# Two-stream transformer blocks in split float32: modulation slabs in a ring of their own, and both halves of the rows in one 512-column product

## The chip, the cores and the metric

One core of a Trainium2 chip runs the kernel. The metric is the device time of one execution in microseconds. The kernel before took 2739.88 us (median of 3 runs, 2738.51 to 2742.72).

## What is computed

Two blocks of two layers each, over 256 latent rows (`x`) and 256 context rows (`ctx`) of width 1024, all in float32. The first block, cut to what matters:

```python
for l in range(2):
    m_lat = split(silu(c) @ ada_w[l] + ada_b[l], 6)          # the same for ctx from c_ctx
    h_lat, h_ctx = modulate(x_lat, m_lat[0], m_lat[1]), modulate(x_ctx, m_ctx[0], m_ctx[1])
    y = even_mixer(...) if l == 0 else odd_mixer(...)        # attentions, then @ w_out
    x_lat = layer_norm(ALPHA * x_lat + m_lat[2] * y_lat, ln_g[l, 0], ln_b[l, 0])
    f = conv_ffn(modulate(x_lat, m_lat[3], m_lat[4]), ...)   # @ w_up, width-3 conv, silu(g) * a, @ w_down
    x_lat = layer_norm(ALPHA * x_lat + m_lat[5] * f, ln_g[l, 1], ln_b[l, 1])
    # x_ctx likewise, in layer 0 only
```

The second block takes these rows and a second context. Each of its layers has RMS norms and modulation with rows of its own, a mixer that adds three gated branches (a 31-tap convolution, differential attention `a = p0 - lam * p1; a @ v`, a multiscale pool), then `@ w_out` and a gated feed-forward `(silu(g) * a) @ w_down`. In layer 0 of each block both streams are computed (512 rows), in layer 1 the latent rows alone (256). The output is the 256 latent rows.

## The kernel before

**Layout.** Activations lie feature by feature: a chunk is 128 features by up to 512 rows. A linear is a list of groups; one group makes 128 output features of all rows in one PSUM bank, from 8 chunks of input (22 in the `down` linears). `plan_linears` writes the order of all linears by hand; `Linear` holds name, groups, tiles to a slab and rows `n`.

**Split products.** Weights and activations are float32, and each is split into a high part, rounded to the matmul's `fp32r`, and a low part, the rest. A product is three matmuls into one bank, high x high, low x high and high x low (lines 570 to 572):

```python
pe.matmul(out, wh[:, cols], high, start=first, stop=False)
pe.matmul(out, wh[:, cols], low, start=False, stop=False)
ins = pe.matmul(out, wl[:, cols], high, start=False, stop=last)
```

**Weights.** SP loads slabs (512 KB, 8 tiles of 128x128; 6 or 5 tiles in `down`) in the order of the plan into a `ring` of four slots. It asks for slab n when slab n-4 has been multiplied (line 526). For each slab ACT copies the high part (line 984) and VectorE subtracts for the low part (line 1617); both do so two slabs ahead (`ahead`, called by `turns` before a group's body). Where the next linear of the plan is one of modulation rows, the look ahead ends, and `begin` makes its successor's first two slabs: in `modulate` at step 3 (`BEGIN`) for `up2_0` and `up2_1`, after the attention for `branch_0` and `branch_1`.

**Groups.** Groups alternate between banks 0 and 1. A body on ACT or VectorE waits for `slab_done`, empties the bank and raises `emptied`; TensorE waits for that before it uses the bank again. `gated` with `residual` serves `mix1` and `down1`, `plain` serves `out` and `down2`, `silu_half`, `high_hidden` and `hidden` serve `up2`. The first two groups of a linear (`opening`) run side by side, chunk by chunk, as their inputs arrive.

**Modulation.** The rows `silu(c) @ w` come in parts named block_layer_part, each 16 slabs of 512 KB. `mod_slab` multiplies one (line 618): four float32 products of 256 columns in four column groups of the array. A part is then copied (`mod_copy`, line 1035), turned by TensorE (`mod_turn`, line 641) and stored with its bias (`mod_store`, line 1634); `stored` makes TensorE wait for that. Parts 1_0_1 and 1_0_2 run between the units of attention `global`, 1_1_0 and 1_1_1 in `near`, 1_1_2 and 2_0_0 in `window`, 2_0_1 and 2_0_2 in `diff_0`, 2_1_1 in `diff_1`. 2_1_0 is multiplied between `out_0` and `up2_0`, 2_1_2 between `out_1` and `up2_1`, through the same ring of four slots. `mods_until` spreads the slabs over the units.

**Attention.** `attend` exists on three engines. A unit is a head pair (or, in `diff`, a head's two maps) by 128 queries: TensorE makes scores (line 719), VectorE the row maxima (1858), ACT the exponentials with their sums (1270), VectorE scales by the reciprocals (1877, 1878; in `diff` 1880 to 1882), TensorE transposes (729), ACT copies (1281), TensorE multiplies by the values (742, 744), VectorE stores (1886). TensorE runs its scores two units ahead, and its modulation slabs between scores and transposes.

**Seams.** After `mix1_0` comes the layer norm `first_norm`: the sum of rows, centring (1717), squares (1059), their sum by TensorE (649), root (1064), reciprocal (1782), then for each chunk the norm (1819), gain and modulation (1241 on ACT, 1822 on VectorE), the high half (1234) and the low half (1663). After `out_0` and `out_1` comes `square_stat`, a root and reciprocal, the update of X (2210, 2215), squares (1564) with TensorE's sums of them (649), a second root and reciprocal, and `modulate` (1676, 1101, 1112, 1694). There TensorE's order is written out by hand: two slabs, `square_stat`, six slabs, then a sum and a slab in turn, eight times.

## Time and profile before

| | |
|---|---|
| median of 3 runs | 2739.88 us |
| the profiled execution | 2742.61 us |
| its span, first to last instruction | 2740.8 us |
| mean granted TensorE clock over the span | 0.974 |
| TensorE busy, share of the span | 94% |
| VectorE, ACT, GpSimd busy | 60%, 46%, 8% |
| DMA, mean over the span | 144 GB/s |

Busy time of TensorE counts every matmul from its start to its modelled end, and matmuls overlap: where they follow each other, the distance of two starts is the cost of one, not its duration. A float32 matmul (scores, slabs, transposes, sums) shows as two records, an `fp32r` one as one. The name before a line number is the engine, then output<-inputs by the kernel's names. In brackets stands the idle time of the engine before the row, and what ended it.

From the first product of a linear to its last, by the timeline, in us:

| stretch | from | to |
|---|---|---|
| attentions `global`, `near` | 151.5 | 282.18 |
| `mix1_0` | 282.18 | 328.31 |
| `up1_0` | 347.65 | 598.19 |
| attention `window` | 777.66 | 856.69 |
| `up1_1` | 921.74 | 1051.70 |
| `down1_1` | 1052.06 | 1116.19 |
| attention `diff_0` | 1465.01 | 1556.68 |
| `out_0` | 1655.88 | 1699.65 |
| `up2_0` | 1738.32 | 1979.03 |
| attention `diff_1` | 2354.91 | 2409.86 |
| `out_1` | 2473.98 | 2499.63 |
| `up2_1` | 2531.51 | 2660.77 |
| `down2_1` | 2661.13 | 2724.78 |

### The profile page before, as it was taken

How to read it: one execution, taken by the hardware profiler on the slowest of the kernel's cores; microseconds unless marked ns; L12 is line 12 of the kernel's file. 1: busy time of each engine (PE TensorE's matmuls, PEld its weight loads, DVE VectorE, ACT ScalarE, POOL GpSimd, SP SyncE). 2: the span in 40 equal slices, each digit the busy share in tenths (PEclk: the TensorE clock that was granted, in tenths of full speed). 3: DMA queues.
4: the chain of work that ended last, by engine and by line, in shares of the span. 5: the costliest groups of instructions: out<-in, count | busy, mean ns of one | idle time of the engine just before them, and what ended most of it. 6: DMA issues, size and time to landing. Idle time of an engine off the chain costs nothing.

```text
span 2740.8 us, 43247 instructions
## 1 busy us (share of the span) xinstructions
PE 2564.3 (94%) x16774; PEld 2154.4 (79%) x16774; DVE 1635.2 (60%) x2702; ACT 1274.2 (46%) x2372; POOL 209.5 (8%) x218
## 2 busy tenths in 40 slices
PE   7989889999988999999999999899999999987997
PEld 4744668888956899988875686588889999685997
DVE  2466465553687686668756763433326788764554
ACT  3355353433656665633336733422235644753443
POOL 3000100001201000324000001000001130000000
PEclk9999999999999999999999999999999999998999
DMA  7267222324554455534324433323245555445555
GB/s 277 86 228 270 72 66 95 99 88 127 164 190 157 149 182 172 175 101 146 115 92 143 140 100 135 125 93 99 88 112 162 170 172 175 154 135 200 176 173 142
DMA packets 119418, 393.64 MB, mean 144 GB/s; under 512 B 13728, under 2 KB 15776, under 8 KB 119136
## 3 DMA queue, kind: packets, MB, share of 16 engines
q1 hardware_dynamic: 117392, 386.47, 44.2%
q0 software_dynamic: 1872, 5.02, 0.7%
q8 instruction: 108, 1.77, 0.3%
q14 instruction: 46, 0.38, 0.0%
HBM read 390.39 MB, written 1.05 MB: 143 GB/s over the span
## 4 chain that ended last, share of the span: by engine, by line
PE 81%; DVE 9%; ACT 4%; DMA 4%; issue 1%; POOL 1%; SPq 0%; ACTq 0%; DVEq 0%; POOLq 0%
PE bank L570 23%; PE bank L571 23%; PE bank L572 23%; PE bank L719 2%; DMA ring<-in_w_mod 2%; PE bank L618 2%; DVE w_low L1617 2%; PE bank L729 2%; PE bank L649 1%; ACT w_high L984 1%; PE bank L744 1%; PE bank L742 1%; DVE smax L1858 1%; DVE conv_space L2118 1%; PE bank L679 1%
## 5 line engine op out<-in xcount | busy, mean ns | idle before, releaser
L570 PE MATMUL bank<-h_high,w_high 128*128 128x256 f32 (+1 forms) x3168 | 1058.4, 334 | 72.7 <-DVE w_low L1617 36.7
L1617 DVE TENSOR_TENSOR w_low<-ring,w_high 128x1024 fp32r<-128x1024 f32 (+2 forms) x604 | 684.1, 1134 | 610.5 <-ACT w_high L984 608.6
L572 PE MATMUL bank<-h_high,w_low 128*128 128x256 f32 (+1 forms) x3168 | 1041.1, 329 | 0.0
L571 PE MATMUL bank<-h_low,w_high 128*128 128x256 f32 (+1 forms) x3040 | 997.5, 328 | 0.0
L570 PEld LDWEIGHTS bank<-h_high,w_high 128*128 128x128 f32 x3168 | 610.8, 193 | 135.1 <-issue 58.3
L984 ACT CAST w_high<-ring 128x1024 fp32r<-128x1024 f32 (+2 forms) x604 | 574.1, 953 | 284.2 <-DMA ring<-in_w_down 161.6
L572 PEld LDWEIGHTS bank<-h_high,w_low 128*128 128x128 f32 x3168 | 610.7, 193 | 51.0
L571 PEld LDWEIGHTS bank<-h_low,w_high 128*128 128x128 f32 x3040 | 585.9, 193 | 48.9 <-issue 0.7
L570 PE MATMUL bank<-f_high,w_high 128*128 128x256 f32 (+1 forms) x880 | 269.2, 306 | 2.7 <-DVE w_low L1617 2.5
L571 PE MATMUL bank<-f_low,w_high 128*128 128x256 f32 (+1 forms) x880 | 267.7, 304 | 0.0
L572 PE MATMUL bank<-f_high,w_low 128*128 128x256 f32 (+1 forms) x880 | 267.6, 304 | 0.0
L570 PEld LDWEIGHTS bank<-f_high,w_high 128*128 128x128 f32 x880 | 168.1, 191 | 10.9 <-DVE w_low L1617 3.6
L571 PEld LDWEIGHTS bank<-f_low,w_high 128*128 128x128 f32 x880 | 168.1, 191 | 7.0
L572 PEld LDWEIGHTS bank<-f_high,w_low 128*128 128x128 f32 x880 | 168.1, 191 | 6.9
L1270 ACT ACTIVATE h_space<-bank,smax 128x512 f32<-128x512 f32 (+1 forms) x192 | 116.3, 610 | 88.8 <-DVE smax L1858 88.5
L2118 DVE SCALAR_TENSOR_TENSOR conv_space<-big,vec,conv_space 128x512 f32<-128x512 f32 (+1 forms) x240 | 150.4, 672 | 1.3
L1389 ACT ACTIVATE conv_space<-bank,vec 128x512 f32<-128x512 f32 (+1 forms) x88 | 59.1, 672 | 180.3 <-PE bank L572 179.1
L1858 DVE TENSOR_REDUCE smax<-bank 128x1 f32<-128x512 f32 (+1 forms) x192 | 108.5, 598 | 40.0 <-PE bank L719 37.0
L618 PE MATMUL bank<-ring,cvec_padded 128*8 128x256 f32 x1408 | 103.5, 392 | 17.7 <-DMA ring<-in_w_mod 16.0
L2011 DVE SCALAR_TENSOR_TENSOR conv_space<-bank,vec,conv_space 128x510 f32<-128x510 f32 (+1 forms) x88 | 54.2, 616 | 102.8 <-ACT conv_space L1389 102.8
L618 PEld LDWEIGHTS bank<-ring,cvec_padded 128*8 128x8 f32 x1408 | 25.4, 88 | 105.2 <-issue 57.3
L570 PE MATMUL bank<-o_halves,w_high 128*128 128x512 f32 (+1 forms) x256 | 91.3, 357 | 13.1 <-DVE w_low L1617 6.7
(230 smaller groups left out, 2625.2 us busy)
## 6 DMA issues: line engine op xcount, KB each, us to landing
ring<-in_w_mod SPq DMA_DIRECT2D x176, 512.0 KB, 4.4
ring<-in_w_up SPq DMA_DIRECT2D x176, 512.0 KB, 3.5
ring<-in_w_down SPq DMA_DIRECT2D x80, 384.0 KB, 3.1
ring<-in_w_down SPq DMA_DIRECT2D x80, 320.0 KB, 3.0
ring<-in_w_gate SPq DMA_DIRECT2D x48, 512.0 KB, 3.5
ring<-in_w_k SPq DMA_DIRECT2D x32, 512.0 KB, 3.5
ring<-in_w_v SPq DMA_DIRECT2D x32, 512.0 KB, 3.5
ring<-in_w_q SPq DMA_DIRECT2D x24, 512.0 KB, 3.5
```

Of the source, the lines that this page charges most:

```text
L570: pe.matmul(out, wh[:, cols], high, start=first, stop=False)
L571: pe.matmul(out, wh[:, cols], low, start=False, stop=False)
L572: ins = pe.matmul(out, wl[:, cols], high, start=False, stop=last)
L618: ins = pe.matmul(bank[b][32 * q:32 * q + MOD_ROWS, 0:256], padded[:, first:first + MOD_ROWS], slab[:, 256 * q:256 * (q + 1)], start=(k == ...
L719: pe.matmul(banks[(2 * u + i) % 4][:, 0:units[u]["T"]], q, k, start=True, stop=True).then_inc(sc_done, 1)
L729: ins = pe.transpose(bank[5 + k % 2][:, t * P:(t + 1) * P], src[:, t * P:(t + 1) * P], IDENT)
L984: nc.scalar.copy(wh[:, cols], raw[:, cols]).then_inc(high_ready, 1)
L1270: nc.scalar.activation(PROB[j % 6][:, 0:unit["T"]], banks[j % 4][:, 0:unit["T"]], ACT.Exp, bias=m, accum_out=ssum[:, j % NS:j % NS + 1]).t ...
L1389: nc.scalar.activation(SC[:, at.u, 0:w], bank[at.u % 2][:, 0:w], ACT.Identity, scale=vcol(l, at.g + (V1["conv_w"] + 2 * FC)), bias=vcol(l, ...
L1617: v.tensor_tensor(wl[:, cols], raw[:, cols], wh[:, cols].bitcast(F32), ALU.subtract).then_inc(low_ready, 1)
L1858: ins = v.reduce_max(m, sc[:, 0:w], AX_X, negate=True)
L2118: ins = v.scalar_tensor_tensor(cvs(c), U[:, c, 0:ns, k:k + S], vcol(l, V2["conv_w"] + c * CONV_TAPS + k), cvs(c), ALU.mult, ALU.add)
```

## The change

**A second ring.** `spare`, eleven slots of a slab in the region that the gates and hidden rows use at other times, takes the slabs of four modulation parts: 1_1_0, which leaves `near`; 2_1_1, which leaves `diff_1`; 2_1_0 and 2_1_2. `plan_spare` gives each slab a slot and names the ring load behind which SP issues it. 1_1_0 is multiplied between `mix1_0` and `up1_0`, 2_1_0 and 2_1_1 between `out_0` and `up2_0`, 2_1_2 where it was. 1_0_2 moves from `global` to `near`. Their turns and stores stand behind `up1_0` and `up2_0`, that of 2_1_2 between the sums.

**Casts ahead.** The four parts leave the plan, so `ahead` reaches from `out_0` and `out_1` into `up2`, and from `group_1` into `branch_1`; `BEGIN` goes. `branch_0`'s first slabs are made in the last unit of `diff_0`.

**`diff`.** The probabilities are `p0 + (s0 * -lam / s1) * p1`, and 1/s0 is applied when the output is stored.

**`first_norm`.** VectorE makes the low half of chunk c-2, not c-1, behind the norm of chunk c.

**Packed products.** In `down1_1`, `up2_1` and `down2_1` the high weights of all groups but the first two meet high and low rows, 256 each, in one product of 512 columns; low weights meet the high rows in the first 256 columns. ACT copies the second half of the bank out, VectorE adds it to the first, then the old body follows.

```diff
+        self.packed = name in ("down1_1", "up2_1", "down2_1")
...
-    modulation(1, 1, 0, 1)
+    modulation(1, 1, 1)
...
-        modulation(2, l, *((1, 2) if l == 0 else (1,)))
+        if l == 0:
+            modulation(2, l, 1, 2)
-        if l == 1:
-            modulation(2, 1, 2)
-        if l == 0:
-            modulation(2, 1, 0)
...
+SPARE = 11
+def plan_spare():
+    order, loads = {}, {}
+    uses, last = [0] * SPARE, [0] * SPARE
+    for parts, places in ((("1_1_0",), [("mix1_0", g, 3) for g in (4, 5, 6)] + [("mix1_0", 7, 2), ("up1_0", 3, 5)]),
+                          (("2_1_0", "2_1_1"), [("merge_0", g, 1) for g in (5, 6, 7)] +
+                           [("out_0", g, 2) for g in (4, 5, 6, 7)] + [("up2_0", 3, 21)]),
+                          (("2_1_2",), [("merge_1", g, 1) for g in (5, 6, 7)] +
+                           [("out_1", g, 2) for g in (4, 5, 6, 7)] + [("up2_1", 3, 5)])):
+        slabs = iter([(part, k) for part in parts for k in range(16)])
+        slot = 8
+        for name, g, count in places:
+            for _ in range(count):
+                one = next(slabs)
+                uses[slot] += 1
+                order[one] = (len(order) + 1, slot, uses[slot], last[slot])
+                last[slot] = len(order)
+                loads.setdefault((name, g), []).append(one)
+                slot = (slot + 1) % SPARE
+    return order, loads
+    SPARE_ORDER, SPARE_LOADS = plan_spare()
...
-    return min(slabs, u * slabs // (len(units) - 2))
+    return min(slabs, u * slabs // (len(units) - (2 if units[0]["diff"] else 0)))
...
+    for one in SPARE_LOADS.get((L.name, at.g), ()) if isinstance(at.g, int) else ():
+        _, slot, _, freed = SPARE_ORDER[one]
+        if freed:
+            sp.wait_ge(spare_done, freed)
+        sp.dma_start(spare[:, slot * SLAB * P:(slot + 1) * SLAB * P],
+                     T["w_mod" + one[0]][one[1] // 4, one[1] % 4]).then_inc(spare_landed[slot], 16)
...
-    if L.halved_at(at.u):
+    if side_by_side(at):
+        both = rhs(kc, at)
+        wide = bank[at.u % 2][:, 0:2 * L.n]
+        if first:
+            pe.matmul(wide, wh[:, cols], both, start=True, stop=False)
+            pe.matmul(out, wl[:, cols], both[:, 0, :], start=False, stop=False)
+        else:
+            pe.matmul(out, wl[:, cols], both[:, 0, :], start=False, stop=False)
+            ins = pe.matmul(wide, wh[:, cols], both, start=False, stop=last)
+    elif L.halved_at(at.u):
...
-        layer_norm(w)
+        spare_slabs("1_1_0", range(3))
+        row_stat(0, w, KC, 2)
+        spare_slabs("1_1_0", range(3, 5))
+        stat(lambda c: O[:, c, 0:w], KC, w, sq_ready, 3)
+        spare_slabs("1_1_0", range(5, 16))
-    linear(f"down1_{l}", of_f(w), arriving=(hid_ready, n["hid"]))
+    if l == 0:
+        mod_turn("1_1_0")
+    linear(f"down1_{l}", both_f if l == 1 else of_f(w), arriving=(hid_ready, n["hid"]))
+        stored()
...
+    def out_norm(c):
+        if l == 0 and c < 6:
+            spare_slabs("2_1_0" if c == 0 else "2_1_1", (15,) if c == 0 else (c - 1,))
+        elif l == 1 and c < 4:
+            spare_slabs("2_1_2", (12 + c,))
+        elif l == 1 and c == 6:
+            mod_turn("2_1_2")
-    mod_rows(part, range(2))
+    spare_slabs(part, range(2))
-    mod_rows(part, range(2, 8))
-    stat(lambda c: QK[:, 8 + c, 0:w], KC, w, sq_ready, 3, lambda c: mod_slab(part, 8 + c))
-    if l == 1:
-        mod_turn("2_1_2")
-    linear(f"up2_{l}", of_h(w), arriving=coming())
+    spare_slabs(part, range(2, (15, 12)[l]))
+    stat(lambda c: QK[:, 8 + c, 0:w], KC, w, sq_ready, 3, out_norm)
+    if l == 0:
+        spare_slabs("2_1_1", range(5, 16))
+    linear(f"up2_{l}", both_h if l == 1 else of_h(w), arriving=coming())
+        mod_turn("2_1_1")
-    linear(f"down2_{l}", of_f(w), arriving=(hid_ready, n["hid"]))
+    linear(f"down2_{l}", both_f if l == 1 else of_f(w), arriving=(hid_ready, n["hid"]))
+        stored()
...
+    def full(at, summed_too=True):
+        act.wait_ge(slab_done, at.full())
+        if side_by_side(at):
+            nc.scalar.copy(TMP[:, at.u % 2, S:TOK], bank[at.u % 2][:, S:TOK]).then_inc(moved, 1)
+            if summed_too:
+                act.wait_ge(summed, at.g + (SUMS[at.L.name] - 1))
+        elif (name, 15) in SPARE_ORDER:
+            act.wait_ge(spare_done, SPARE_ORDER[name, 15][0])
...
-        if u == half and len(beside) == 2:
+        if len(beside) == 2 and u == halfway[0]:
+        if opens is not None and u == len(units) - 1:
+            begin(LIN[opens], ahead)
-    mod_copy(beside[-1])
+    if beside:
+        mod_copy(beside[-1])
...
-    attend(f"diff_{l}", square_out)
+    attend(f"diff_{l}", square_out, opens="branch_0" if l == 0 else None)
-    begin(LIN[f"branch_{l}"], ahead)
...
+    def add_halves(at):
+        dve.wait_ge(moved, at.g + (SUMS[at.L.name] - 1))
+        out = bank[at.u % 2][:, 0:S]
+        v.tensor_tensor(out, out, TMP[:, at.u % 2, S:TOK], ALU.add).then_inc(summed, 1)
...
+    if side_by_side(at):
+        add_halves(at)
...
-    if c:
-        low(lambda _: HL[:, c - 1, :], lambda _: O[:, c - 1, :], lambda _: HH[:, c - 1, :], 1, TOK)
+    if c == 1:
+        low_normed(0)
+    elif c > 2:
+        low_normed(c - 2)
...
-    own.inc(v.tensor_tensor(r1, r1, lam, ALU.mult))
-    own.link(v.tensor_scalar(p0, p0, r0, None, ALU.mult))
+    s0 = ssum[:, j % NS:j % NS + 1]
+    own.link(v.scalar_tensor_tensor(r1, s0, lam, r1, ALU.mult, ALU.mult))
-    v.tensor_copy(units[u]["out"], OUTB[:, 0:P]).then_inc(o_ready, 1)
+    if units[u]["diff"]:
+        r0 = srec[:, 2 * u % NS:2 * u % NS + 1]
+        v.tensor_scalar(units[u]["out"], OUTB[:, 0:P], r0, None, ALU.mult).then_inc(o_ready, 1)
+    else:
+        v.tensor_copy(units[u]["out"], OUTB[:, 0:P]).then_inc(o_ready, 1)
...
+    if l == 1:
+        mod_store("2_1_2")
-    L = LIN[f"up2_{l}"]
-    if l == 1:
-        mod_store("2_1_2")
-    modulate(l, 2 + l, 1, 24, ns, True, L)
+    modulate(l, 2 + l, 1, 24, ns, True)
...
+    if side_by_side(at):
+        add_halves(at)
-        dve.wait_ge(slab_done, at.full())
+        if side_by_side(at):
+            dve.wait_ge(summed, at.g + (SUMS["up2_1"] - 1))
+        else:
+            dve.wait_ge(slab_done, at.full())
```

## Rows read from the trace of the kernel before

**Rows 1.** The page: the chain by engine; from the costliest groups, ACT's casts.
```profile
PE 81%; DVE 9%; ACT 4%; DMA 4%; issue 1%; POOL 1%; SPq 0%; ACTq 0%; DVEq 0%; POOLq 0%
L984 ACT CAST w_high<-ring 128x1024 fp32r<-128x1024 f32 (+2 forms) x604 | 574.1, 953 | 284.2 <-DMA ring<-in_w_down 161.6
```

**Rows 2.** Timeline of TensorE in `up1_0`, then in `up2_1`; start, us, instruction.
```profile
400.31 0.39 PE L570 MATMUL bank<-h_high,w_high 128*128 128x512 f32 x1
400.54 0.39 PE L571 MATMUL bank<-h_low,w_high 128*128 128x512 f32 x1
...
2600.17 0.28 PE L572 MATMUL bank<-h_high,w_low 128*128 128x256 f32 x1
2600.29 0.28 PE L570 MATMUL bank<-h_high,w_high 128*128 128x256 f32 x1
```

**Rows 3.** Windows: us; busy PE, PEld, DVE, ACT, POOL; PEclk, DMA share, GB/s.
```profile
12.00:24.00 12.00, 8.16 (x80) 1.17 (x80) 0.86 (x5) 1.39 (x3) 0.00 (x0) 1.00 1.03 410
1700.33:1738.32 37.99, 21.80 (x149) 5.29 (x149) 23.75 (x34) 14.98 (x25) 0.00 (x0) 0.82 0.67 235
2499.99:2531.51 31.52, 18.52 (x155) 5.87 (x153) 14.58 (x33) 10.16 (x22) 0.00 (x0) 0.82 0.79 286
2544.00:2661.13 117.13, 117.13 (x978) 117.13 (x977) 64.55 (x83) 55.88 (x84) 0.00 (x0) 1.00 0.57 180
```

**Rows 4.** Waits (us, times, longest) in `global`, in `near`, in `diff_0`.
```profile
PE bank L618 <- DMA ring<-in_w_mod: 3.5, 4, 1.5
...
PE bank L618 <- DMA ring<-in_w_mod: 2.8, 5, 0.7
...
PEld bank L729 <- DVE h_space L1882: 10.4, 16, 1.0
```

**Rows 5.** Timeline: slabs and a turn in `global`, then a unit of `diff_1`.
```profile
190.19 1.05 PE L618 MATMUL bank<-ring,cvec_padded 128*8 128x256 f32 x16
194.27 1.48 PE L618 MATMUL bank<-ring,cvec_padded 128*8 128x256 f32 x24
...
214.54 0.62 PE L641 MATMUL bank<-pick,conv_space 128*128 128x16 f32 x4 [0.35 <-DVE mod L1634]
...
2382.66 0.48 DVE L1881 TENSOR_SCALAR h_space<-h_space,srec 128x512 f32<-128x512 f32 x1
2383.12 1.13 PE L719 MATMUL bank<-qk 64*128 64x512 f32 x4
2386.20 0.70 PE L719 MATMUL bank<-qk 64*128 64x512 f32 x2
```

**Rows 6.** Timeline: first products of two chunks of `up1_0`.
```profile
358.42 0.50 PE L570 MATMUL bank<-h_high,w_high 128*128 128x512 f32 x1 [1.29 <-DVE h_low L1663]
...
360.89 0.50 PE L570 MATMUL bank<-h_high,w_high 128*128 128x512 f32 x1 [0.82 <-DVE h_low L1663]
```

**Rows 7.** Timeline of the seam before `up2_0`: slabs, root, first chunk, first product.
```profile
1704.09 0.62 PE L618 MATMUL bank<-ring,cvec_padded 128*8 128x256 f32 x8 [0.15 <-DMA ring<-in_w_mod]
...
1711.38 1.04 PE L618 MATMUL bank<-ring,cvec_padded 128*8 128x256 f32 x8 [1.46 <-DMA ring<-in_w_mod]
...
1725.74 0.69 ACT L1064 ACTIVATE rstd<-bank,small 128x512 f32<-128x512 f32 x1 [6.30 <-PE bank L649]
...
1733.26 0.69 DVE L1694 TENSOR_TENSOR h_low<-l_space,h_high 128x512 fp32r<-128x512 f32 x1 [1.45 <-ACT h_high L1112]
...
1738.32 0.76 PE L570 MATMUL bank<-h_high,w_high 128*128 128x512 f32 x1 [12.07 <-DVE w_low L1617]
```

**Rows 8.** Timeline of the seam before `up2_1`: the root, the first product.
```profile
2522.18 0.47 ACT L1064 ACTIVATE rstd<-bank,small 128x256 f32<-128x256 f32 x1 [11.27 <-PE bank L649]
...
2531.51 0.55 PE L570 MATMUL bank<-h_high,w_high 128*128 128x256 f32 x1 [7.65 <-DVE w_low L1617]
```

**Rows 9.** Timeline: a copy in `down2_1`, an addition in a bank in `near`.
```profile
2725.34 0.37 ACT L1138 COPY h_space<-bank 128x256 f32<-128x256 f32 x1 [3.97 <-PE bank L572]
...
263.89 0.42 DVE L1856 TENSOR_TENSOR bank<-bank,big 128x256 f32<-128x256 f32 x1
```

More of the change, by code:

```diff
@@ L472, in build @@
             MODS[name] = (6, SC[:, 7, :], 6)
-        BESIDE = {"global": ("1_0_1", "1_0_2"), "near": ("1_1_0", "1_1_1"), "window": ("1_1_2", "2_0_0"),
-                  "diff_0": ("2_0_1", "2_0_2"), "diff_1": ("2_1_1",)}
+        BESIDE = {"global": ("1_0_1",), "near": ("1_0_2", "1_1_1"), "window": ("1_1_2", "2_0_0"),
+                  "diff_0": ("2_0_1", "2_0_2"), "diff_1": ()}
         def columns_of(name):
@@ L1114, in modulate @@
                         begin(L, ahead, (step,))
-                    elif L is not None and rooted and step == BEGIN:
-                        begin(L, ahead)
             def gain(ln, vl, c, w):
@@ L1255, in attend @@
                 banks, probt = (DIFF_SCORES, PROBT) if diff else (PAIR_SCORES, PAIR_PROBT)
-                half = next(u for u in range(len(units)) if mods_until(units, 16 * len(beside), u) >= 16)
+                halfway = [u for u in range(len(units)) if mods_until(units, 16 * len(beside), u) >= 16]
                 j0, u0, t0 = n["sub"], n["unit"], n["turned"]
@@ L1687, in modulate @@
                         begin(L, ahead, (step,))
-                    elif L is not None and rooted and step == BEGIN:
-                        begin(L, ahead)
                     c = step - lag - 2
@@ L1900, in attend @@
                         finish(c)
+                    if opens is not None and units[u]["diff"] and u == len(units) - 1:
+                        begin(LIN[opens], ahead)
                 store(len(units) - 1)
@@ L1903, in attend @@
                 n["unit"] += len(units)
-                if opens is not None:
+                if opens is not None and not units[0]["diff"]:
                     begin(LIN[opens], ahead)
@@ L2028, in _ @@
                 n["fh"] += FC
+                if l == 0:
+                    mod_store("1_1_0")
                 dve.wait_ge(x_ready, n["x"])
```

70 lines of the change are left out of this document (46 added, 24 removed).

## The prediction

> **What bounds the kernel now.** The page comes first: TensorE holds 81% of the chain that ended last, and the casts of weights on ACT wait mostly for the down slabs' DMA [rows 1]. So time leaves this kernel in two ways: fewer TensorE passes where it runs without a gap, or shorter stretches where it waits. The starts of single products tell what a pass costs: a 512-column one starts 0.227 us after the one before it (400.54 less 400.31), a 256-column one 0.12 us (2600.17 to 2600.29) [rows 2]. The difference, 0.107 us, is 256 columns at the 2.4 GHz level; what is left of either, 0.013 us, is what each product costs beside its columns. Then the windows by stage [rows 3]: in `up2_1` TensorE is busy for all 117.13 us, so passes saved there come off the time; in the seams before `up2_0` and `up2_1` (37.99 and 31.52 us) it is busy for a little over half. What ends the waits in the stretches of the sum is in rows 4 to 8.
>
> **The attentions.** `global` has 32 modulation slabs, two or three a unit, and after the change 16. Three slabs (24 records) lasted 1.48 us and two 1.05 [rows 5], so one more costs 0.43: 6.9 us for 16. TensorE itself waited 3.5 us for slabs there [rows 4]; with half of the traffic I take all of it as gone. One turn of modulation rows leaves, 0.62 us and 0.35 of waiting for the store [rows 5]: 1.0. Together 11.4 us; bounds 6.9 and 16, the latter if the units then run at their shorter engine's pace. In `near` the 32 slabs stay, but are spread over 16 units instead of 14; TensorE waited 2.8 us for them [rows 4]: 2.0, and 1.0 in `window`, which has the same new spread; bounds nothing and 5.
>
> `diff_1` loses its 16 slabs. Its scores start every 3.08 us (2383.12, 2386.20) [rows 5]. Alone a slab costs between 0.43 and the 0.62 us of its records; at 0.54 TensorE needs 2.55 us without it. VectorE drops the 0.48 us pass that scales the first probabilities [rows 5], as the reciprocal moves into the store of the output, which it makes anyway; so it does not take over as the bound. I take 2.68 us a unit, 0.13 over TensorE's need for the coupling: 16 x 0.4 = 6.5 us, bounds 3 and 9. `diff_0` keeps a slab a unit. TensorE's weight loads waited 10.4 us there, 16 times, for the pass that VectorE now makes without its predecessor [rows 4]; some of that is hidden by running products. I take 4.5 us, bounds nothing and 10. The casts for `branch`, moved into or ahead of the attention, I take at nothing: they stand beside the last units' work; without that cover they would cost about 2 us each time, two casts and two subtractions of half a slab.
>
> **The norm before `up1_0`.** Now VectorE makes chunk c, waits for the high half of c-1, and only then makes c+1: the first products of two chunks start 2.47 us apart (358.42, 360.89), and TensorE waited before both [rows 6], while a chunk is six products of 0.227, 1.36 us. With the low half one chunk later VectorE is the limit: two passes like the one of 0.69 us in rows 7 and one of half the width every second chunk, about 1.6 us. Over eight chunks 2.6 less 1.6 is 8 us; I take 7.5, as the slabs that now stand in this seam delay the first sum by 0.4; bounds 4 and 9. The 16 slabs themselves (6.9 us of TensorE) stand beside centring, squares and reciprocal; without that cover they cost their 6.9. 11 are loaded in `mix1_0`, whose slabs last 5.44 us each (24 x 0.227): up to four loads in that time, where the fastest stretch moved 410 GB/s, 1.28 us a slab [rows 3]. It fits.
>
> **The seam before `up2_0`.** The root is asked for at 1725.74. Two of the eight slabs between the sums leave, 1.1 us, and the first sum no longer stands behind the slab of 1711.38 and its 1.46 us of waiting, 2.5 with it [rows 7]: 3.6 us. The casts for `up2_0`'s first slabs leave the seam, being made during `out_0`: the first product waited for their low halves until 1738.32, where the first chunk's low half was ready at 1733.95 [rows 7]: 4.4 us. Against these 8 stand 32 slabs instead of 16. 11 are there; 21 and one ring slab land after 1700.3: 22 x 1.28 = 28.2 us behind some 2 of latency, so the last is multiplied near 1731.8 and sets the start. 6.5 us are left; bounds 8, and a loss of 4.3 (a rival).
>
> **The seam before `up2_1`.** The root came at 2522.18 [rows 8], held up by slabs between the sums, not by squares. With 11 of 16 slabs there, four of the rest beside the first sums and none beside the others, I work out 2514: 8.2 us. The modulation store stands before the reciprocal now, not behind it: 0.7. The first product waited for low halves of weights until 2531.51 [rows 8]; without the casts in front it follows the first chunk, 3.6 us sooner, as in the other seam. 12.5 us; bounds 8 and 14. The granted clock was 0.82 in both seams' windows [rows 3], partly the 1.2 GHz level after waits; I give no gain to it. Two more turns of modulation rows, after `up1_0` and `up2_0`, cost 0.62 us each [rows 5]: 1.2 back. SP's queue gets 64 issues ahead of ring loads. Those that wait for a slot stand behind a linear's fourth slab, and the ring slot asked for next is freed only when that linear runs, so nobody waits for SP.
>
> **The packed products.** `down1_1`, `up2_1` and `down2_1` have 176, 352 and 176 chunk products of three matmuls; without each one's first two groups 132 + 336 + 132 = 600. Three at 0.12 are 0.36 us; one at 0.12 and one at 0.227 are 0.347: 600 x 0.0133 = 8.0 us. Added in each of 54 groups are an ACT copy (0.37 us) and a VectorE addition in the bank (0.42) [rows 9], and two handovers. Behind ACT's new wait stand its next cast and the bank's release. In `up2_1` the other bank's group lasts 8 x 0.347 = 2.8 us, and copy, addition, silu and handovers some 1.6: hidden, at nothing. In the down linears ACT's cast waited for DMA anyway [rows 1] and now starts about as late for another reason: 0.1 us in 12 groups, 1.2. At the ends of `down1_1` and `down2_1` nothing hides the pair: 0.9 us each. 8.0 less 3.0 is 5.0 us; bounds 8 and a loss of more. Whether a 512-column product whose moving operand lies in two pieces runs at 0.227 no row shows. I take the price of the contiguous one, the nearest of that width and type; above it I go to the double, below it to nothing.
>
> Rows 2 say that a product with its weight load costs 0.013 us beside its columns. The Trainium skill (TensorE: Matmul & The Clock Gate, The mechanism) says that loads overlap running matmuls only where the row group differs, and the same page's section on LDWEIGHTS gives 128 columns at 1.2 GHz, 107 ns; by that, an estimate from the page, 600 loads fewer would save 64 us, not 8. The trace disagrees: with a load each, products start 0.12 us apart.
>
> **Sum.** 11.4 + 2.0 + 1.0 + 6.5 + 4.5 + 7.5 + 6.5 + 12.5 - 1.2 + 5.0 = 55.7 us. The profiled execution took 2742.6 us around a span of 2740.8; its forecast is 2686.9. It lies 2.7 above the median of 2739.9, which gives 2684.
>
> **Rivals.** (a) The sum, within 15 us: 0.68. (b) DMA sets the seam before `up2_0`: four slabs took from 1704.09 to 1711.38 there, 1.8 us each [rows 7]. 22 x 1.8 = 40 us, `up2_0` starts at 1742.6, 4.3 later instead of 6.5 sooner, and `mix1_0` and `out_1` lose 3: 2698. For: the stretch moved 235 GB/s, not 410 [rows 3]. Against: a ring of four slots limited it. 0.12. (c) Bank handover decides in `up2_1`: with a cast of 0.95 us [rows 1] and a subtraction of about that before copy and addition, the chain of 1.6 becomes 3.7, 0.9 over the other group's time; 42 x 0.9 = 38, 2722. Against: both engines are busy for half of the window [rows 3]. 0.05. (d) The attentions run at their shortest engine: 4.6 more in `global`, 2.5 in `diff_1`, 5.5 in `diff_0`, and a clock that stays up in the seams, 5: 2666. 0.09. (e) Slower: the two-piece operand streams slower. From 0.32 us a wide product (0.227 + 56/600) all gain is gone; at the double, 0.45, it is 2684 + 600 x 0.227 = 2820. 0.03. (f) A load costs a whole 0.12: the packing saves 72 us, not 8: 2620, nearly excluded by rows 2. The page's rule above is this one. 0.01. (g) The change doesn't do what it says: the wide product is issued as two of 256 columns with two loads; nothing is saved, the additions stay: 2692. 0.02.
>
> **Numbers.** Forecast 2684. The range of 8 in 10 is (a) with most of (b), (d) and (g): 2666 to 2705. A measurement of this kernel tells about 0.2%, 5.5 us, from no change. Faster: all but (e), less a remainder for several misses at once, 0.95; within 0.2%: 0.02; slower: 0.03.
>
> **What would show it.** `up2_1` some 4 us shorter, starts alternating between 0.12 and 0.227; `diff_1` units of 2.6 to 2.7; first products of `up1_0`'s chunks 1.6 apart; the wait before `up2_0` ended by a slab, the one before `up2_1` by a low half of h. Waits for the addition in front of products in `up2_1`, or starts over 0.3 after a wide product, would prove it wrong.

## The result and the profile after

The changed kernel takes 2700.61 us (median of 4 runs, 2700.26 to 2702.05) against 2739.7 us before: ratio 0.9857, 95% interval 0.984 to 0.9874, so 39.1 us faster. The forecast was 2684, in a range of 2666 to 2705. The direction and the range held, and 39 of the 56 us came. Its profiled execution took 2700.43 us around a span of 2698.6; set against that of before (2742.61) the gain is 42.2 us, and the table is made against this. One execution of one kernel below (the casts for `up2` in the seam) took 3149.86 us at a mean granted clock of 0.761, where its four others took 2709 to 2714 us; it is left out of the times, and as it was the profiled one, that kernel has no profile to set beside the rest.

In the changed kernel the three products of 256 columns stand at L620 to L622, and the packed pair at L616 (low weights) and L617 (high weights, 512 columns; L613 for a group's first). First its page: the chain by engine, then ACT's casts of weights (busy us, mean ns, idle before them).

```profile
PE 80%; DVE 9%; ACT 4%; DMA 4%; issue 2%; POOL 1%; SPq 0%; ACTq 0%; DVEq 0%; POOLq 0%
L1061 ACT CAST w_high<-ring 128x1024 fp32r<-128x1024 f32 (+2 forms) x604 | 574.6, 953 | 260.5 <-DMA ring<-in_w_down 150.8
```

The chain looks as in [rows 1]: no other engine has become the bound of the whole. So the stages must be read one by one. The table comes from the timelines of TensorE of both kernels: a stretch runs from the last product of one linear to the first of the next, or over the products of a linear.

| Stretch | before, us | after, us | gain | forecast |
|---|---|---|---|---|
| `global` | 72.7 | 60.9 | 11.8 | 11.4 |
| `near` | 67.6 | 65.2 | 2.4 | 2.0 |
| `window` | 88.4 | 88.9 | -0.5 | 1.0 |
| seam and `up1_0` (the norm) | 269.9 | 262.6 | 7.3 | 7.5 |
| two more turns | 1.7 | 2.5 | -0.8 | -1.2 |
| `diff_0` | 93.1 | 89.9 | 3.2 | 4.5 |
| seam before `up2_0` | 38.7 | 34.4 | 4.3 | 6.5 |
| `diff_1` | 56.0 | 51.7 | 4.3 | 6.5 |
| `out_1` | 25.7 | 29.3 | -3.6 | 0 |
| seam before `up2_1` | 31.9 | 19.9 | 12.0 | 12.5 |
| `up2_1` and `down2_1`, to the end | 209.3 | 208.0 | 1.3 | 5.0 |
| `down1_1` and the wait behind it | 64.8 | 66.1 | -1.4 | in the 5.0 |

These sum to 40.3; the other 1.9 us lie in stages whose products did not change. The table sets one profile of each kernel against the other, and a stage whose instructions are the same can differ between two profiles, by 4.3 us at most in what follows; so a row of 1 or 2 us says little by itself. Next the windows of the changed kernel, with the columns of [rows 3]: a stretch inside `diff_1`, then `up2_1`, then the two seams.

```profile
2340.00:2372.00 32.00, 30.97 (x200) 20.78 (x199) 30.88 (x75) 26.87 (x84) 0.00 (x0) 1.00 0.00 1
...
2494.00:2617.00 123.00, 122.01 (x704) 106.24 (x704) 81.16 (x129) 75.37 (x133) 0.00 (x0) 1.00 0.55 178
1677.50:1711.80 34.30, 29.52 (x280) 8.95 (x278) 21.61 (x32) 12.10 (x22) 0.00 (x0) 0.92 0.87 337
...
2470.70:2490.56 19.86, 14.35 (x158) 6.92 (x156) 14.27 (x31) 8.32 (x21) 1.14 (x1) 0.94 0.45 160
```

In the seam before `up2_0` the DMA share went from 0.67 to 0.87 and the rate from 235 to 337 GB/s: its slabs now set its length. Both seams have the granted clock at 0.92 and 0.94, where [rows 3] have 0.82. In `diff_1` VectorE is now busy for 30.88 of 32 us.

The timeline of the changed kernel, first ACT in `out_1`, then the ends of the two seams (start, us, instruction, idle time before it and what ended it):

```profile
2457.01 1.05 ACT L1061 CAST w_high<-ring 128x1024 fp32r<-128x1024 f32 x1 [2.26 <-DMA ring<-in_w_out]
2461.83 1.05 ACT L1061 CAST w_high<-ring 128x1024 fp32r<-128x1024 f32 x1 [3.21 <-DMA ring<-in_w_out]
2469.49 1.05 ACT L1061 CAST w_high<-ring 128x1024 fp32r<-128x1024 f32 x1 [2.22 <-DMA ring<-in_w_up]
...
1702.30 0.69 ACT L1153 ACTIVATE rstd<-bank,small 128x512 f32<-128x512 f32 x1 [5.06 <-PE bank L702]
1709.82 0.69 DVE L1791 TENSOR_TENSOR h_halves<-l_space,h_halves 128x512 fp32r<-128x512 f32 x1 [1.45 <-ACT h_halves L1201]
1710.84 1.04 PE L668 MATMUL bank<-spare_slabs,cvec_padded 128*8 128x256 f32 x8 [0.33 <-DMA spare_slabs<-in_w_mod]
1711.81 0.79 PE L620 MATMUL bank<-h_halves,w_high 128*128 128x512 f32 x1
...
2485.71 0.47 ACT L1153 ACTIVATE rstd<-bank,small 128x256 f32<-128x256 f32 x1 [1.36 <-PE bank L702]
2490.56 0.55 PE L620 MATMUL bank<-h_halves,w_high 128*128 128x256 f32 x1 [4.88 <-DVE h_halves L1791]
```

The seam before `up2_0` ends with a slab's landing at 1710.84, and the one before `up2_1` with a low half of h, both as the prediction said. What it did not say is at the top: in `out_1` ACT waits for its own ring slabs, queued behind spare ones.

### The profile page after: what moved, and what is told of

The parts are those of the page before. It is cut to its first block, busy times and chain, and to the rows that moved or that the text cites. A ratio compares the mean times of both kernels' runs of the same rounds, so it can differ in the third digit from the quotient of the medians.

```text
span 2698.6 us, 42207 instructions
## 1 busy us (share of the span) xinstructions
PE 2551.6 (95%) x16174; PEld 2120.8 (79%) x16174; DVE 1641.4 (61%) x2708; ACT 1291.3 (48%) x2426; POOL 212.9 (8%) x218
## 4 chain that ended last, share of the span: by engine, by line
PE 80%; DVE 9%; ACT 4%; DMA 4%; issue 2%; POOL 1%; SPq 0%; ACTq 0%; DVEq 0%; POOLq 0%
PE bank L620 21%; PE bank L621 20%; PE bank L622 20%; PE bank L617 3%; PE bank L772 2%; DVE w_low L1710 2%; PE bank L668 2%; PE bank L782 2%; PE bank L616 2%; ACT w_high L1061 2%; DVE smax L1963 1%; PE bank L702 1%; PE bank L797 1%; DMA ring<-in_w_down 1%; DVE conv_space L2231 1%
## 5 line engine op out<-in xcount | busy, mean ns | idle before, releaser
L620 PE MATMUL bank<-h_halves,w_high 128*128 128x256 f32 (+1 forms) x2832 | 961.2, 339 | 52.0 <-DVE w_low L1710 14.1
L622 PE MATMUL bank<-h_halves,w_low 128*128 128x256 f32 (+1 forms) x2832 | 944.7, 334 | 0.0
L621 PE MATMUL bank<-h_halves,w_high 128*128 128x256 f32 (+1 forms) x2704 | 900.8, 333 | 0.0
L620 PEld LDWEIGHTS bank<-h_halves,w_high 128*128 128x128 f32 x2832 | 545.1, 192 | 113.7 <-issue 34.8
L622 PEld LDWEIGHTS bank<-h_halves,w_low 128*128 128x128 f32 x2832 | 545.1, 192 | 50.9
L621 PEld LDWEIGHTS bank<-h_halves,w_high 128*128 128x128 f32 x2704 | 520.0, 192 | 48.8 <-issue 0.7
L620 PE MATMUL bank<-f_halves,w_high 128*128 128x256 f32 (+1 forms) x616 | 194.6, 316 | 2.3 <-DVE w_low L1710 2.1
L621 PE MATMUL bank<-f_halves,w_high 128*128 128x256 f32 (+1 forms) x616 | 192.9, 313 | 0.0
L622 PE MATMUL bank<-f_halves,w_low 128*128 128x256 f32 (+1 forms) x616 | 192.9, 313 | 0.0
L620 PEld LDWEIGHTS bank<-f_halves,w_high 128*128 128x128 f32 x616 | 117.3, 190 | 10.5 <-DVE w_low L1710 2.7
L621 PEld LDWEIGHTS bank<-f_halves,w_high 128*128 128x128 f32 x616 | 117.4, 191 | 7.1
L622 PEld LDWEIGHTS bank<-f_halves,w_low 128*128 128x128 f32 x616 | 117.4, 191 | 6.8
L617 PE MATMUL bank<-h_halves,w_high 128*128 128x512 f32 x294 | 104.8, 396 | 0.0
L620 PE MATMUL bank<-o_halves,w_high 128*128 128x512 f32 (+1 forms) x256 | 90.2, 352 | 12.2 <-DVE w_low L1710 5.5
L1677 ACT ACTIVATE conv_space<-bank 128x512 f32<-128x512 f32 (+1 forms) x44 | 21.6, 492 | 143.0 <-PE bank L622 129.0
```

The costliest lines, as they stand in the source:

```text
L617: ins = pe.matmul(wide, wh[:, cols], both, start=False, stop=last)
```

## The experiments

Each kernel is the changed one with one edit, except the last, which starts from the kernel before, and the two ahead of it, which keep `branch_1`'s casts late as well. The diffs are cut to what matters. Times of different sets are compared by their ratio to the kernel before, run beside them; 0.001 is 2.7 us. The changed kernel's own ratio, run again in the second set, is 0.985.

**Without packing.**

```diff
-        self.packed = name in ("down1_1", "up2_1", "down2_1")
+        self.packed = False
```

> Nothing is packed; all else as in the changed kernel. Theory A (from its trace): a packed product takes 0.350 us where three of 256 columns take 0.360, so 600 of them save 6.0 us, and the two down linears and their ends give nearly all of what is saved there and in up2_1 back: this kernel comes out at 2700 to 2702 us (measured changed kernel: 2700.6), with up2_1 at 129.3 us instead of 126.75, down1_1 at 64.1 instead of 65.2 and down2_1 at 63.65 instead of 64.3. Rival B (the forecast's own term): the packing is worth 5.0 us, so this one takes 2705.5 us. Rival C: the addition costs more than is seen in up2_1, and this kernel is faster than the changed one by over 2 us, below 2698.5.

Measured: 2696.86 us, ratio 0.9833 (0.9819 to 0.9847). `up2_1` took 128.6 us, `down1_1` 65.6, `down2_1` 63.0. The forecast's +5 (rival B) is refuted. Theory A's total is missed too, but less clearly: the kernel is better without its packing by 0.0017, 4.7 us, as rival C has it, and the two intervals overlap (the last experiment has a narrower one).

**Packing in `up2_1` alone.**

```diff
-        self.packed = name in ("down1_1", "up2_1", "down2_1")
+        self.packed = name == "up2_1"
```

> Only up2_1 is packed, the two down linears are not. Theory A: up2_1 keeps its 2.5 us, down1_1, down2_1 and what follows each give back 2.8 to 3 us together (1.1 and 0.3 around down1_1, 0.7 and 0.7 around down2_1): 2697.8 us. Rival B: the down linears gain 0.5 us net by the packing, as the forecast has them, and this kernel takes 2701.1 us.

Measured: 2694.72 us, ratio 0.9825 (0.9811 to 0.9838), below what A and B expected. That is 2.1 us below the kernel without any, inside the noise of the two, and its `up2_1` is 2.1 us shorter (126.5 against 128.6). Against the kernel with all three the two down linears cost 0.0025, 6.9 us, where their own stages, with what follows them, show 2.8. What happens inside the stage is in the timeline of the changed kernel's `down1_1`:

```profile
1057.43 0.48 ACT L1135 ACTIVATE tmp<-bank,mod 128x256 f32<-128x256 f32 x1 [1.16 <-DVE bank L1719]
1057.80 0.82 ACT L1061 CAST w_high<-ring 128x768 fp32r<-128x768 f32 x1
1059.22 0.73 ACT L1061 CAST w_high<-ring 128x640 fp32r<-128x640 f32 x1 [0.59 <-DMA ring<-in_w_down]
...
1060.22 0.38 PE L616 MATMUL bank<-f_halves,w_low 128*128 128x256 f32 x1 [0.48 <-DVE w_low L1710]
```

ACT waits 1.16 us for VectorE's addition (L1719), its next cast starts behind that, the one after it waits for its slab as well, and TensorE waits for low halves of weights in the middle of a group. Such places (0.2 to 0.7 us of pitch beyond the usual) come four times in `down1_1`. They are not the packing's alone: the kernel without packing has three waits of this kind there, 2.4 us in all, with no addition to wait for. Over all profiles `down1_1` took 65.0 to 65.8 us packed (eight profiles) and 64.1 to 65.6 us not packed (five profiles), 0.8 us less on the mean; `down2_1` took 62.8 to 64.3 and 63.0 to 63.7, 0.2 us less on the mean.

**One piece instead of two.** The low half of a chunk is stored behind its high half; the products are the same.

```diff
-                return HB[:, :, kc, 0:S]
+                return HH[:, kc, 0:2 * S]
...
-                return FB[:, :, kc, 0:S]
+                return FH[:, kc, 0:2 * S]
```

> The same products, but the low half of a chunk is stored right behind its high half, so that the moving operand of the 512-column product is one run of 512 columns. Theory D: the two pieces are what makes such a product take 0.234 us where a 512-column one elsewhere takes 0.227; then wide and narrow start 0.347 us apart, 336 products in up2_1 save 1.0 us (125.8 us), 600 in all 1.8 us: 2698.8 us. Rival E: the pieces cost nothing, and the 0.003 us more come from something else (the alternation of widths): 0.350 stays, 2700.6 us.

Measured: 2702.39 us, ratio 0.9851 (0.9835 to 0.9866). TensorE's timeline in its `up2_1`:

```profile
2559.89 0.40 PE L617 MATMUL bank<-h_halves,w_high 128*128 128x512 f32 x1
2560.14 0.28 PE L616 MATMUL bank<-h_halves,w_low 128*128 128x256 f32 x1
2560.26 0.40 PE L617 MATMUL bank<-h_halves,w_high 128*128 128x512 f32 x1
```

and that of the changed kernel:

```profile
2559.97 0.40 PE L617 MATMUL bank<-h_halves,w_high 128*128 128x512 f32 x1
...
2560.20 0.28 PE L616 MATMUL bank<-h_halves,w_low 128*128 128x256 f32 x1
...
2560.32 0.40 PE L617 MATMUL bank<-h_halves,w_high 128*128 128x512 f32 x1
```

Over the 252 pairs inside the groups of `up2_1` a wide product is followed after 0.2341 us and a narrow one after 0.116 in both kernels: 0.350 together. Theory D is refuted, and E holds: an operand in these two pieces streams as fast as one in a single run. A pair is worth 0.010 us over three products (0.36), not the 0.0133 of [rows 2].

**Fewer spare loads in `out_1`.**

```diff
-                           [("out_1", g, 2) for g in (4, 5, 6, 7)] + [("up2_1", 3, 5)])):
+                           [("out_1", g, 1) for g in (4, 5, 6, 7)] + [("up2_1", 3, 9)])):
```

> In out_1, one spare slab is loaded behind each of the last four ring slabs instead of two; the other four are loaded in the seam before up2_1. Theory F: out_1 grew from 25.65 to 29.27 us because its own and up2_1's first ring slabs queue behind the spare ones at 1.28 us each; with four of them fewer out_1 takes 26 to 27 us, while the seam's last slab lands about 5 us later after out_1's end, so the seam grows from 19.9 to 23 to 25 us; in all 2700 to 2703 us. Rival G: the casts for up2_1 ahead of their time are what holds out_1 up, and it stays at 29 us or more; then the total is 2703 to 2706 us.

Measured: 2703.54 us, ratio 0.9854 (0.9839 to 0.9869). `out_1` fell to 24.9 us and the seam before `up2_1` grew to 26.5. ACT in its `out_1`:

```profile
2464.79 1.05 ACT L1061 CAST w_high<-ring 128x1024 fp32r<-128x1024 f32 x1 [1.79 <-DMA ring<-in_w_out]
...
2469.82 1.05 ACT L1061 CAST w_high<-ring 128x1024 fp32r<-128x1024 f32 x1 [0.89 <-DMA ring<-in_w_up]
```

The longest wait for `out_1`'s own slabs fell from 3.2 to 1.8 us. Theory F holds (both stages moved its way, and by more than it had) and G falls: the queue of slabs is what lengthened `out_1`, and its bytes are paid either there or in the seam.

**The low half first, as before.**

```diff
-                    if c == 1:
-                        low_normed(0)
-                    elif c > 2:
-                        low_normed(c - 2)
+                    if c:
+                        low_normed(c - 1)
```

> In the norm before up1_0, VectorE makes the low half of chunk c-1 right behind chunk c again, as the kernel before does; all else as changed. Theory H: this order alone gives the 7.8 us by which up1_0 became shorter (250.55 to 242.72), so up1_0 takes 250 to 251 us and the kernel is 7.8 us slower than the changed one. Rival I: the eleven and five slabs put into the seam before up1_0 shift the work so that the order hardly matters; then up1_0 stays within 2 us of 242.7.

Measured: 2707.62 us, ratio 0.9864 (0.9848 to 0.9879); `up1_0` 248.9 us, 6.2 more. The window over its first 10 us, of this kernel and then of the changed one:

```profile
334.00:344.00 10.00, 7.79 (x24) 5.28 (x24) 5.12 (x9) 5.51 (x11) 0.00 (x0) 0.84 0.01 2
```

```profile
334.00:344.00 10.00, 9.82 (x36) 7.82 (x36) 8.67 (x16) 8.83 (x18) 0.00 (x0) 0.83 0.01 2
```

24 products in 10 us against 36. The order is worth 6.2 us of `up1_0`, where H had 7.8, and 3.8 us of the whole by ratio (5.2 by medians), where H had 7.8 too. Rival I falls; H is right about the cause and too high in the price.

**Scaling the first probabilities again.**

```diff
-                    own.link(v.scalar_tensor_tensor(r1, s0, lam, r1, ALU.mult, ALU.mult))
+                    own.inc(v.tensor_tensor(r1, r1, lam, ALU.mult))
+                    own.link(v.tensor_scalar(p0, p0, r0, None, ALU.mult))
...
-                        v.tensor_scalar(units[u]["out"], OUTB[:, 0:P], r0, None, ALU.mult).then_inc(o_ready, 1)
+                    v.tensor_copy(units[u]["out"], OUTB[:, 0:P]).then_inc(o_ready, 1)
```

> In the two diff attentions VectorE scales the first probabilities in a pass of its own again and stores the output with a plain copy. Theory J: in diff_1 VectorE is the bound of the changed kernel (30.9 us busy of 32 at 2.57 us a unit), so 0.41 us more a unit (0.48 less the 0.07 that the scaled store costs over the copy) come out whole: units of 2.98 us, 5.3 to 6.5 us in diff_1, and 3 us in diff_0, 8 to 10 us in all. Rival K: only the slabs that left made the units shorter, and TensorE has the slack; then diff_1 grows by under 2 us and the total by under 3.

Measured: 2706.51 us, ratio 0.9862 (0.9847 to 0.9877): 3.3 us by ratio, 4.1 by medians, where J had 8 to 10; the intervals overlap. `diff_1` 55.3 us (3.6 more), `diff_0` 94.0 (4.1 more than in the changed kernel's first profile, 2.6 more than in its second, where that stretch took 91.4). Inside its `diff_1`:

```profile
2345.00:2375.00 30.00, 27.52 (x170) 17.32 (x167) 29.28 (x74) 22.29 (x69) 0.00 (x0) 1.00 0.00 1
```

VectorE is busy for 29.28 of 30 us, and a unit takes 2.85 us instead of 2.57. J is right about the engine and too high in the price (0.28 us a unit, not 0.41). A unit took 3.09 us before, so of the 0.52 us saved the folded pass gives 0.28 and the slabs that left 0.24. That the stretch still takes 55.3 us here, against 56.0 before, is also due to 3.2 us that moved casts cost in it, as the run with late casts shows.

**The changed kernel again.**

> The changed kernel once more, beside the others on one chip. Theory A (packing is worth nothing in all, and what differs in other stages is the clock of single executions): within 1.5 us of the kernel without packing of the first set, when each is set against the kernel before: ratio 0.983 to 0.985. Rival C (packing costs time in all): its ratio is 0.985 to 0.987, 4 to 8 us above the one without packing.

Measured: 2702.46 us, ratio 0.985 (0.9837 to 0.9864), at the border of the two expectations, 0.0017 above the one without packing.

**The casts for `up2` in the seam.**

```diff
-                        ahead(at.later(j + AHEAD_SLABS))
+                        later = at.later(j + AHEAD_SLABS)
+                        if not (later is not None and L.name.startswith("out") and later[0].L.name.startswith("up2")):
+                            ahead(later)
...
+                    elif L is not None and rooted and step == 3:
+                        begin(L, ahead)
```

> The casts and subtractions for up2's first two slabs stand in the seam again, behind the fourth chunk, and not in out's last groups. Theory L: the seam before up2_1 grows by 3.6 us and the one before up2_0 by 3 us (there the slabs' DMA would end it at 34.4 us anyway, so of the 4.4 us only what goes beyond it counts), while out_1, whose last ACT copies now wait behind a cast that waits for DMA, gives back 1 us: 5 to 6 us slower than the changed kernel. Rival M: both seams are set by their slabs, and the casts are hidden wherever they stand: under 2 us.

Measured: 2713.67 us (four runs, 2708.72 to 2714.08), ratio 0.989 (0.9875 to 0.9905): 11 us slower, twice what L expected. M is refuted. Where the other 5 us arise stays open.

**`branch_1`'s casts late.** They stand in `diff_1`'s last unit again.

```diff
-                if l == 1:
-                    begin(LIN["branch_1"], ahead)
-                attend(f"diff_{l}", minus_lam, opens="branch_0" if l == 0 else None)
+                attend(f"diff_{l}", minus_lam, opens=f"branch_{l}")
...
-                        ahead(at.later(j + AHEAD_SLABS))
+                        if L.name != "group_1":
+                            ahead(at.later(j + AHEAD_SLABS))
```

> The changed kernel with branch_1's first casts back inside diff_1 (in its last unit, as branch_0's are), instead of ahead of it through group_1. Theory N: in the changed kernel ACT's two casts wait for branch_1's slabs in front of the last two silu copies that free the banks for the scores, and diff_1's first scores come 3.3 us after group_1's last product instead of 1.0; so here they come at 1.0 again, diff_1 is 2.3 us shorter, 49.4 us from group_1 to branch_1 instead of 51.7, and the total is 2 us lower. Rival O: the time comes back at the other end, where the casts stand in front of branch_1 (its first product waited 2.5 us for them in the kernel before): no gain, 51.5 us.

Measured: 2698.65 us, ratio 0.9843 (0.9826 to 0.986), 1.9 us less by ratio, which the intervals do not show by themselves, and 48.5 us from `group_1` to `branch_1`, 3.2 less. The start of `diff_1` in the changed kernel:

```profile
2327.07 0.62 ACT L1061 CAST w_high<-ring 128x512 fp32r<-128x512 f32 x1 [1.67 <-DMA ring<-in_w_branch]
2327.59 0.47 ACT L1596 ACTIVATE conv_space<-bank,vec 128x256 f32<-128x256 f32 x1
...
2329.09 1.99 PE L772 MATMUL bank<-qk 64*128 64x512 f32 x8 [2.94 <-ACT conv_space L1596]
```

and with the casts late:

```profile
2330.57 0.91 ACT L1597 ACTIVATE conv_space<-bank,vec 128x256 f32<-128x256 f32 x2 [0.36 <-PE bank L625]
...
2331.62 1.99 PE L773 MATMUL bank<-qk 64*128 64x512 f32 x8 [0.66 <-ACT conv_space L1597]
```

A cast that waits for a slab stood in ACT's order between the silu copies that free the banks for the scores. The first scores come after a wait of 0.66 us instead of 2.94. N holds, O falls: the stretch shows it in both profiles with late casts (48.5 us each).

**The same without packing.**

```diff
-        self.packed = name in ("down1_1", "up2_1", "down2_1")
+        self.packed = False
```

> The same as the run beside it, without the packing. Theory A (the packing is worth nothing in all by its own stages): within 1.5 us of that run. Rival C (the kernel without packing is faster, by 4 to 6 us, as the first two sets of runs have it, because the stretches from od_q to k_0_ctx run at a lower granted clock with it): 4 to 6 us less than that run, with od_q at 24.5 us instead of 26.8. Rival B (the forecast's term): 5 us more than that run.

Measured: 2696.05 us, ratio 0.9827 (0.9809 to 0.9845): again 0.0016 (4.4 us by ratio, 2.6 by medians) better without packing. B is out; the intervals of this pair do not decide between A and C. C's reason did not come as stated: `od_q` took 25.8 us here, not 24.5, and 27.2 us in the run beside it.

**The parts that gained.** This one has `branch_1`'s casts late, packing in `up2_1` alone, and the halves in one piece.

```diff
-        self.packed = name in ("down1_1", "up2_1", "down2_1")
+        self.packed = name == "up2_1"
...
-                return HB[:, :, kc, 0:S]
+                return HH[:, kc, 0:2 * S]
```

> Packing in up2_1 alone, its two halves in one run of 512 columns, and the branch casts late: the parts that gained, without those that lost. If they add up, up2_1 is 126 us, diff_1 49.4 us, od_q 24.5 us: 2.5 us below the run without packing and 6 to 8 us below the changed kernel, a ratio of 0.982 to the kernel before. If the gains are of the clock's chance only, it stays at 0.984 to 0.985.

Measured: 2694.53 us, ratio 0.9822 (0.9804 to 0.9839). It beats the kernel before clearly and the changed one by 0.0028 or 8 us; against the run without packing it gains 0.0005, less than the noise, where 2.5 us were expected. Its `up2_1` is 126.2 us and `diff_1` 48.5, but `od_q` 27.6.

**Packing alone, on the kernel before.** The kernel before with the hunks of the diff that make the packed product, the copy (`full`) and the addition (`add_halves`).

> The kernel before with the packing of the three linears and nothing else of the change. Theory A: up2_1 becomes 2.5 us shorter, the down linears with what follows them 2 to 2.5 us longer: within 1.5 us of the kernel before. Rival B (the forecast): 5.0 us faster. Rival C: 4 us slower.

Measured: 2748.27 us (12 runs) against 2743.37 (17 runs), ratio 1.0017, interval 1.0007 to 1.0027. The packing by itself makes the kernel slower by 4.7 us, clear of the measurement. Rival C holds; A and B are out. Its `up2_1` is 2.9 us shorter, as A had it, `down1_1` with the wait behind it 1.5 us longer, and the end behind `down2_1` 0.7. So the loss is not in the packed stages. Its one profile (2752.44 us, 9.8 more than the profile before) has 4.3 us of the difference in `global` and `near` (144.7 against 140.4) and 3.3 in `window` (91.7 against 88.4). The edit touches no instruction there and moves no buffer.

## Why the prediction was right in direction and short in size

**The forecast as a whole.** The range held, but the result lies 16.6 us above 2684, just outside the 15 us of rival (a), since nearly all misses point one way. Rival (b) has the nearest time, 2698, and is not what happened: the seam before `up2_0` gained 4.3 us where (b) had it lose as much, and only its loss in `out_1` came. The starts in `up2_1` do alternate, between 0.116 and 0.234 us; it became 2.5 us shorter, not 4.

**Right, with their terms.** `global` and `near` (14.2 us against 13.4), the norm (7.3 against 7.5) and the seam before `up2_1` (12.0 against 12.5) are 33.5 of the 42 us. For `global` and `near` no run took the change back; the same instructions took 126.0 to 128.9 us in eleven profiles, so the gain is 11.5 to 14.3 against the 140.4 before. The norm's size is in part luck. The chunks' first products in the changed kernel:

```profile
338.60 0.39 PE L620 MATMUL bank<-h_halves,w_high 128*128 128x512 f32 x1
...
339.97 0.39 PE L620 MATMUL bank<-h_halves,w_high 128*128 128x512 f32 x1
```

They come 1.37 us apart, TensorE's own six products, so VectorE is not the limit at 1.6 us that the prediction made of it; the first two chunks took 2.67 and 1.75, in part at the 1.2 GHz level, for which the prediction gave nothing. From the first product to the 49th, behind the eighth chunk, `up1_0` took 20.98 us before, 14.74 after and 21.01 with the low half first: 6.2 us, of which the later start (19.9 us behind `mix1_0` instead of 19.3) takes 0.5. The other 1.6 us are no part of the change: the packing alone, with the old order, has `up1_0` at 249.0 us, where the kernel before had 250.5.

In the seam before `up2_1` the root came 15.0 us behind `out_1`'s last product (2485.71 less 2470.70) where it had been 22.6 [rows 8]. The seams' clock also rose from 0.82 to 0.92 and 0.94, for which I had given nothing.

**The packed products: the step that failed.** The prediction said 600 x 0.0133 = 8.0 us, less 3.0 for the additions. The second factor measured 0.010, so 6.0: a 512-column product between narrow ones is followed after 0.234 us, not after 0.227. The costs were sized too low as well. "0.1 us in 12 groups" is single stalls of 0.2 to 0.9 us, some 2 us in each down linear of the changed kernel; from the means over all profiles the packing costs 2.1 us in `down1_1` and 1.5 in `down2_1` beside the 1.3 that each saves. In `up2_1`, where I had nothing, it is 1.3: 2.1 us came on the mean of the 3.4 that 336 products save. Only the ends cost less than forecast, 0.3 and 0.7 us where I had 0.9 each. By their own stages the three linears give -0.1 us in all.

By whole times the packing costs 4.7, 4.4 and 4.7 us in three pairs of kernels, of which the last alone is clear of the noise. What is between is not in the packed stages. The mean granted clock over the runs of each pair is lower with packing: 0.9804 against 0.9834, 0.9804 against 0.9820, 0.9741 against 0.9755. Of 2700 us, 0.0014 to 0.003 of mean clock are 8 to 16 us more at the 1.2 GHz level, 4 to 8 us of time if TensorE sets the pace in all of them. The runs on record do not bear that price out. Among the 101 runs whose clock is listed, compared inside each kernel, 0.001 of mean clock goes with 0.5 us (an estimate from a straight line through them, 0.3 to 0.8), so that the clocks would explain 0.7 to 1.6 us. Why the packing would lower the clock was not shown either. What makes the rest, some 3 to 5 us, stays open.

The rival of the weight load (72 us) is out: the packed kernel issues 600 loads fewer (16174 instead of 16774) and isn't faster for it. With it goes, for this kernel, the Trainium skill's rule that loads overlap only where the row group differs (TensorE: Matmul & The Clock Gate, The mechanism). The same section also lets a load into the background weight buffer run ahead, which the prediction left out; the starts 0.12 us apart with a load each agree with that, and no run here shows which buffer a load goes to.

**`out_1`, the step left out.** The prediction worked out for `mix1_0` that up to four loads fit into a slab's time, and gave `out_1` no such sum and no term. `out_1`'s slabs have 256 columns: a group lasts 64 x 3 x 0.12 / 8 = 2.9 us, and three loads at 1.28 us are 3.8. Its 3.6 us are this (2.8 in the changed kernel's second profile). Rival (b) had named it ("`mix1_0` and `out_1` lose 3"); `mix1_0` lost nothing.

**`diff_1`, the step costed at nothing.** The units are 2.57 us instead of 3.09 in the steady part, 0.52 saved where I took 0.40. But the moved casts, "at nothing", cost 2.3 us at the start and 3.2 in all. With them late the gain is 7.5 us, over the 6.5 forecast. The sentence named the end of the attention as their place; the half that counts stands ahead of it, and I never asked what is queued behind a cast that waits. Also wrong: "so it does not take over as the bound". VectorE has, by the window and by this row of the waits in `diff_1` (us in all, times, longest):

```profile
PEld bank L782 <- DVE h_space L1987: 13.3, 15, 1.5
```

**The seam before `up2_0`.** The mechanism was right (the last slab ends it), the size off by 2.2 us. 22 slabs at 1.28 behind 2 us were to end 31 us after the linear; the last landed 33.4 after it (1710.84 less 1677.45). (The prediction's own figures, 1700.3 + 2 + 28.2, make 1730.5, not the 1731.8 that it goes on with.) Rival (b)'s 1.8 us a slab was wrong: they came at 1.28 near the end, 0.62 of products and 0.66 of waiting. The other path fell short as well: the root came 24.9 us behind `out_0`'s last product (1702.30 less 1677.45) where it had been 26.1, a gain of 1.2 and not of 3.6. The first chunk's low half was ready at 1710.51, so even without the last slab the seam would have ended 1.3 us sooner at most.

**`diff_0`, `window`.** 3.2 of 4.5, within the bounds given; -0.5 of 1.0, just below the bound of nothing. In `window` one profile does not carry the sign: the same instructions took 87.2 us in the kernel without packing, and those of before 91.7 in the packing alone.

## What to carry to other kernels

When work is moved into the shadow of something else, write down for each queue what stands directly behind it: a cast or a load that has to wait costs what is queued after it, not its own time. When a load burst is spread over a linear, divide by that linear's own slab time. And when a change trades an instruction for side work on two engines, run it alone: here it shortened the stage that everyone looks at and made the kernel slower.

## What the runs showed of the hardware

- A 512-column moving operand in two pieces 4096 columns apart costs the same as one run: 0.2341 us to the next product in both kernels, where pure 512-column streams have 0.227. A narrow product after a wide one is followed after 0.116, less than the 0.12 of a pure narrow stream.
- After nearly the same pause TensorE's clock can be at either level. Before `od_q` TensorE waits, and up to there these four kernels have the same instructions. The first product, in the changed kernel, without packing, with packing in `up2_1` alone, and in the parts that gained:

```profile
707.76 0.58 PE L620 MATMUL bank<-h_halves,w_high 128*128 128x256 f32 x1 [3.55 <-DVE h_halves L1893]
```

```profile
707.24 0.39 PE L620 MATMUL bank<-h_halves,w_high 128*128 128x256 f32 x1 [2.98 <-DVE h_halves L1893]
```

```profile
707.80 0.39 PE L620 MATMUL bank<-h_halves,w_high 128*128 128x256 f32 x1 [3.29 <-DVE h_halves L1893]
```

```profile
707.67 0.58 PE L621 MATMUL bank<-h_halves,w_high 128*128 128x256 f32 x1 [3.26 <-DVE h_halves L1895]
```

and the window behind it, in the same order:

```profile
708.00:733.00 25.00, 25.00 (x184) 24.79 (x185) 14.47 (x24) 13.46 (x29) 5.78 (x6) 0.90 0.38 129
```

```profile
708.00:733.00 25.00, 24.46 (x197) 24.08 (x197) 16.22 (x27) 16.33 (x34) 5.79 (x6) 1.00 0.49 148
```

```profile
708.00:733.00 25.00, 24.81 (x200) 24.39 (x199) 16.05 (x26) 16.28 (x34) 5.79 (x6) 1.00 0.45 153
```

```profile
708.00:733.00 25.00, 24.81 (x179) 24.18 (x179) 14.35 (x23) 12.96 (x28) 6.81 (x6) 0.89 0.39 128
```

  After 3.29 us without work the clock stayed at 1.00 and 200 products ran; after 3.26 us it was 0.89 and 179 did. Where it was 0.90, some 5 us of the window ran at 1.2 GHz, and `od_q` took 26.8 us instead of 24.5. So the length of the pause alone does not decide it. The Trainium skill (TensorE: Matmul & The Clock Gate, What's actually happening) says that the gate's watch does not start with the kernel, so the place of a change varies from run to run. The profiles agree: the low clock stands in other stretches from kernel to kernel, and single stages of unchanged instructions differ by up to 4.3 us. Differences of that size are to be read from several runs, not from one profile.
